# Attention with stationary values and sums divided in the transposes, evictions on ScalarE and split mLSTM cells, in a two-layer diffusion trunk

## What is computed

```python
def step(carry, xs):                       # mLSTM, one chunk of 128 tokens, one direction
    C, n, m = carry
    b = jnp.cumsum(fc, axis=-1)
    d = jnp.where(lower, b[..., :, None] - b[..., None, :] + ic[..., None, :], -jnp.inf)
    inter = b + m[..., None]
    m_t = jnp.maximum(inter, jnp.max(d, axis=-1))
    w = jnp.exp(d - m_t[..., None]) * jnp.einsum('bhtd,bhsd->bhts', qc, kc)
    a = jnp.exp(inter - m_t)
    num = a[..., None] * jnp.einsum('bhtd,bhdv->bhtv', qc, C) + jnp.einsum('bhts,bhsv->bhtv', w, vc)
...
def one_block(qblk):                       # attention
    s = jnp.einsum('bkgqd,bksd->bkgqs', qblk, k, preferred_element_type=jnp.float32) * scale
    p = jax.nn.softmax(s, axis=-1).astype(v.dtype)
    return jnp.einsum('bkgqs,bksd->bkgqd', p, v)
...
act = jax.nn.gelu(jnp.einsum('tped,td->tpe', u[eidx], xb), approximate=False)   # PEER
return jnp.einsum('tpe,tped->td', g * act, v[eidx])
```

## Time and profile before

| | before |
|---|---|
| median of 3 runs | 2664.69 us (2655.25 to 2669.79) |
| profiled execution | 2655.81 us, span 2654.0 us |
| TensorE matmuls busy | 1909.4 us (72%) |
| VectorE busy | 1847.1 us (70%) |
| ScalarE busy | 604.0 us (23%) |
| GpSimd busy | 861.5 us (32%) |
| gathers | 110592 packets, 805.36 MB, 74.5% of 16 DMA engines |
| all DMA | 958.15 MB, mean 361 GB/s |
| granted TensorE clock | 0.846 |

### The profile page before, as it was taken

One profiled execution on the slowest core, in us unless ns is written; L12 is line 12 of the kernel. 1 busy time (PEld: TensorE's weight loads), 2 busy tenths in 40 slices (PEclk: granted clock), 3 DMA queues, 4 the chain that ended last, 5 costly groups with the idle time before them and its releaser, 6 DMA issues. The chain is left out here.

```text
span 2654.0 us, 22937 instructions
## 1 busy us (share of the span) xinstructions
PE 1909.4 (72%) x6742; PEld 1103.9 (42%) x6742; DVE 1847.1 (70%) x4569; ACT 604.0 (23%) x1668; POOL 861.5 (32%) x772
## 2 busy tenths in 40 slices
PE   6686687588687666678877667488867776766665
PEld 5466354366354223344534335245534332322222
DVE  1325876686686897166688863988688779687765
ACT  2212322332121221122321221233211112211121
POOL 0001332233323443134334322344333444444432
PEclk8787888799788787678889878799879898888888
DMA  9755798679898999979899978799999999999996
GB/s 404 284 202 238 264 367 327 229 306 371 336 392 358 405 403 387 381 310 421 359 420 420 415 302 340 282 388 387 358 374 421 419 385 421 422 409 422 419 421 266
DMA packets 141040, 958.15 MB, mean 361 GB/s; under 512 B 19701, under 2 KB 21749, under 8 KB 25717
## 3 DMA queue, kind: packets, MB, share of 16 engines
q0 software_dynamic: 110592, 805.36, 74.5%
q1 hardware_dynamic: 23024, 147.01, 14.0%
q10 hardware_dynamic: 7300, 4.33, 0.5%
HBM read 953.75 MB, written 2.89 MB: 360 GB/s over the span
## 5 line engine op out<-in xcount | busy, mean ns | idle before, releaser
L677 PE MATMUL acc<-rows,diag 128*128 128x512 f32 x2136 | 1160.6, 695 | 453.1 <-ACT diag L853 452.7
L608 POOL DMA_INDIRECT rows<-in_uv,eidx x768 | 861.3, 1121 | 1754.0 <-PE acc L677 1220.8
L1135 DVE CUSTOM_DVE_ANT_0 rows<-rows,xb 128x1024 f32<-128x1024 f32 x768 | 917.7, 1222 | 259.6 <-DMA rows<-in_uv,eidx 259.0
L677 PEld LDWEIGHTS acc<-rows,diag 128*128 128x128 f32 x2136 | 454.3, 223 | 1074.8 <-ACT diag L853 571.4
L853 ACT ACTIVATE act_out<-act_in 128x2 f32<-128x2 f32 x384 | 78.1, 203 | 1448.5 <-DVE act_in L1135 1448.2
L1124 DVE SCALAR_TENSOR_TENSOR side<-rows,wv,side 128x1024 f32<-128x1024 f32 x234 | 300.7, 1285 | 8.4
L853 ACT ACT_TABLE_LOAD x138 | 177.1, 1283 | 133.8 <-DVE st L1088 33.7
L626 PE MATMUL bank<-wt,hT 128*128 128x256 f32 x896 | 200.0, 384 | 8.1 <-ACT hT L853 7.5
L853 ACT ACTIVATE diag<-small,wv 128x128 f32<-128x128 f32 x534 | 191.8, 387 | 0.0
L626 PEld LDWEIGHTS bank<-wt,hT 128*128 128x128 f32 x896 | 172.8, 193 | 39.2 <-ACT hT L853 8.1
L626 PE MATMUL bank<-hT,wt 128*128 128x256 f32 (+1 forms) x960 | 179.5, 348 | 4.5 <-ACT hT L853 3.7
(11 more groups left out here) (161 smaller groups left out, 1329.3 us busy)
## 6 DMA issues: line engine op xcount, KB each, us to landing
wt<-in_ada_w SPq DMA_DIRECT2D x27, 1024.0 KB, 10.9
wt<-in_peer_w_q SPq DMA_DIRECT2D x26, 1024.0 KB, 9.5
rows<-in_ada_w SPq DMA_DIRECT2D x21, 1024.0 KB, 19.6
wt<-in_mlstm_w_in SPq DMA_DIRECT2D x14, 1024.0 KB, 7.6
rows<-in_uv,eidx POOLq DMA_INDIRECT x768, 12.9
wt<-in_attn_w_qkv SPq DMA_DIRECT2D x12, 1024.0 KB, 9.5
rows<-in_mlstm_w_in SPq DMA_DIRECT2D x10, 1024.0 KB, 27.6
wt<-in_attn_w_out SPq DMA_DIRECT2D x8, 1024.0 KB, 9.7
```

What stands on the lines that cost most here:

```text
L608: nc.gpsimd.indirect_dma_start(out=rows[:, r, :], out_offset=None, in_=A["uv"], in_offset=bass.IndirectOffsetOnAxis(ap=eidx[:, b, slot:slo ...
L677: last = nc.tensor.matmul(acc[:, h * 512:(h + 1) * 512], diag[:, r, :], rows[:, r, D + h * 512:D + (h + 1) * 512], start=first and j == 0, ...
L1135: last = V.tensor_tensor_reduce(out=rows[:, r, 0:D], in0=rows[:, r, 0:D], in1=xb[:, place, :], scale=1.0, scalar=0.0, op0=ALU.mult, op1=AL ...
```

## The change

In words: (1) NT: both tiles go to ScalarE except for block 0 of layer 0. (2) PS: ScalarE copies the scores. (3) The steps MLA, MLB, MLC become MLD, MLW, MLA / MLB, MLE (two heads each) / MLC, MLK, MLU, with their own unit costs; MLB, MLE and MLU are late on VectorE, MLB and MLE on ScalarE. (4) AQ, a new step, squares q and k on ScalarE. (5) The rotary takes both axes in one operation. (6) A new step AR: VectorE inverts the sums, ScalarE makes a diagonal of each head's; AP is a product of prA with that diagonal; ScalarE copies the result; AV has the values stationary and two heads' probabilities moving, output by feature, which ScalarE copies into hT; T2 of layer 1 keeps only the gate. prA and the diagonals lie in the place of q in qkv.

```diff
@@ plan
-                yield ("MLA", g, d, b)
-                yield ("MLB", g, d, b)
+                yield from ((k, g, d, b) for k in ("MLD", "MLW", "MLA", "MLB", "MLE"))
                 if g == "P" or n < nb - 1:
-                    yield ("MLC", g, d, b)
+                    yield from ((k, g, d, b) for k in ("MLC", "MLK", "MLU"))
...
-        yield from (("AN", g, b) for b in range(nb))
+        for b in range(nb):
+            yield ("AQ", g, b)
+            yield ("AN", g, b)
         yield from (("AT", g, b) for b in range(nb))
-        yield from ((k, g, b, kv) for b in range(nb) for kv in range(AKV) for k in ("AS", "AP", "AV"))
+        yield from ((k, g, b, kv) for b in range(nb) for kv in range(AKV) for k in ("AS", "AR", "AP", "AV"))
@@ cost
-        return {"MLQK": 13, "MLV": 13, "MLO": 13, "OUT": 13, "PQ": 13, "AQKV": 13, "AS": 4, "AP": 5, "AV": 5, "MOD": 10}.get(s[0], 0) / (2 - both) \
-            or {"MLA": 8, "MLG": 8, "MLN": 10, "PS": 4, "PC": 5, "PG": 7, "PT": 5, "AN": 15, "CONV": 6, "NT": 4}.get(s[0], 6)
+        return {"MLQK": 13, "MLV": 13, "MLO": 13, "OUT": 13, "PQ": 13, "AQKV": 13, "AS": 4, "AR": 2, "AP": 5, "AV": 4, "MOD": 10}.get(s[0], 0) / (2 - both) \
+            or {"MLD": 4, "MLW": 4, "MLA": 4, "MLB": 4, "MLE": 5, "MLC": 3, "MLK": 2, "MLU": 5, "MLG": 8, "MLN": 10, "PS": 4, "PC": 5, "PG": 7, "PT": 5, "AQ": 1, "AN": 14, "CONV": 6, "NT": 4}.get(s[0], 6)
@@ in_order
-    late = {"P": (), "A": ("NT", "MLQK", "MLV", "MLO", "AQKV", "PQ", "OUT", "T2", "PS", "AS"),
-            "D": ("NT", "MLQK", "MLV", "MLO", "AQKV", "PQ", "OUT", "T2", "PS", "MOD", "AS", "AP", "AV")}[who]
+    late = {"P": (), "A": ("NT", "MLQK", "MLV", "MLO", "AQKV", "PQ", "OUT", "T2", "PS", "MLB", "MLE", "AS", "AP", "AV"),
+            "D": ("NT", "MLQK", "MLV", "MLO", "AQKV", "PQ", "OUT", "T2", "PS", "MLB", "MLE", "MLU", "MOD", "AS")}[who]
@@ psum_tiles
     if k == "NT":
-        return "AD"
+        return "AD" if nt_shared(s) else "AA"
...
     if k == "PS":
-        return "D" if s[4] else "DAA"
+        return "A" if s[4] else "AAA"
...
     if k == "AP":
-        return "DDDD"
+        return "AAAA"
     if k == "AV":
-        return "D"
+        return "A"
@@ TensorE
                 elif k == "AP":
                     _, g, b, kv = s
                     nk = 1 if g == "P" else 3
+                    pe.wait_ge(sums_diag, next_of(sums_diag))
                     for i in range(4):
-                        transposes(open_tile(i), [prA[i][:, c * P:(c + 1) * P] for c in range(nk)]).then_inc(tile_full, 1)
+                        t = open_tile(i)
+                        for c in range(nk):
+                            last = mm(t[:, c * P:(c + 1) * P], prA[i][:, c * P:(c + 1) * P], dgA[i], True, True)
+                        last.then_inc(tile_full, 1)
                 elif k == "AV":
...
-                    for i in range(4):
+                    for i in range(2):
                         for c in range(nk):
...
-                            last = mm(out[:, i * HD:(i + 1) * HD], prA[i][:, c * P:(c + 1) * P], v, c == 0, c == nk - 1)
+                            pair = qkv[:, 0:2, (3 * i + c) * P:(3 * i + c + 1) * P]
+                            last = mm(out[i * HD:(i + 1) * HD, 0:2 * P], v, pair, c == 0, c == nk - 1)
@@ ScalarE
+                elif k == "AQ":
+                    f(sq20, qkv[:, s[2], 0:(AH + AKV) * HD], ACT.Square).then_inc(squares, 1)
...
+                elif k == "AP":
+                    _, g, b, kv = s
+                    n = P if g == "P" else 3 * P
+                    for i in range(4):
+                        copy_tile(i, prA[i][:, 0:n], n)
+                elif k == "AR":
+                    act.wait_ge(sums_inverted, next_of(sums_inverted))
+                    for i in range(4):
+                        last = f(dgA[i], ident, ACT.Copy, scale=rrs[:, i:i + 1])
+                    last.then_inc(sums_diag, 1)
+                elif k == "AV":
+                    _, g, b, kv = s
+                    copy_tile(0, hT[:, 2 * kv:2 * kv + 2, tok(b)], 2 * P, lambda t: t.rearrange("p (q n) -> p q n", n=P))
@@ VectorE
+                elif k == "AR":
+                    V.reciprocal(rrs, rsum).then_inc(sums_inverted, 1)
```

More of the change, by code:

```diff
@@ L215, in psum_tiles @@
         return "DD"
+    if k == "MLD":
+        return "DD"
     if k == "MLA":
-        return "DDA"
-    if k == "MLB":
-        return "AD" * MH if s[1] == "S" else "D" * MH
+        return "A"
+    if k in ("MLB", "MLE"):
+        return "AD" * 2 if s[1] == "S" else "D" * 2
     if k == "MLC":
-        return "D" * (1 + MH)
+        return "D"
+    if k == "MLU":
+        return "D" * MH
     if k == "T2":
-        return "A" * (2 * len(BLOCKS[s[2]]) + 2)
+        return "A" * (2 * len(BLOCKS[s[2]]) * (s[1] == 0) + 2)
     if k == "OUT":
@@ L321, in needed @@
         return after("T2")
-    if s[0] == "PS" and who != "D":
+    if s[0] == "PS" and who == "P":
         return after("PQ")
@@ L485, in places @@
             for s in PLAN:
-                before.append((len(owner), total["A"], total["D"], total["acts"], total["dves"]))
+                held = {"MLW": 2, "MLA": 1, "MLK": 1}.get(s[0], 0)
+                before.append((len(owner), total["A"], total["D"] - held, total["acts"], total["dves"]))
                 for e in psum_tiles(s):
@@ L497, in begin @@
                 s = PLAN[i]
-                if s[0] in (*IDLE[who], "GROUPS") or (s[0] == "PS" and who == "A" and s[4]):
+                if s[0] in (*IDLE[who], "GROUPS") or (s[0] == "MLU" and who == "A" and s[1] == "S"):
                     return 0, 0, 0, 0, 0
@@ L750, in _ @@
                     last.then_inc(tile_full, 1)
-                elif k == "MLA":
+                elif k == "MLD":
                     _, g, d, b = s
@@ L920, in _ @@
                     c = COND[b]
[L921 to L922 removed]
                     place = tok(b - (b > 0))
[L924 to L927 removed]
+                    for i in range(1 if nt_shared(s) else 2):
+                        act.wait_ge(tile_full, full(i))
+                        t = tile(i)
+                        for q in range(4):
+                            e = 4 * i + q
+                            last = f(hT[:, e, place], t[:, q * P:(q + 1) * P], ACT.Identity,
+                                     scale=gain[:, l, w, e, c:c + 1], bias=modT[:, l, 24 * w + e, c:c + 1])
+                        last.then_inc(act_freed, 1)
                 elif k == "MLQK":
@@ L964, in _ @@
                     last.then_inc(probs_raw, 1)
-                    copy_tile(2, WT.rearrange("p h n -> p (h n)"))
-                elif k == "MLB":
+                elif k == "MLA":
+                    copy_tile(0, WT.rearrange("p h n -> p (h n)"))
+                elif k in ("MLB", "MLE"):
                     if s[1] == "S":
                         act.wait_ge(act_chain, noted())
-                        for h in range(MH):
-                            act.wait_ge(tile_full, full(2 * h))
-                            t = tile(2 * h)
+                        for i in range(2):
+                            h = i + 2 * (k == "MLE")
+                            act.wait_ge(tile_full, full(2 * i))
+                            t = tile(2 * i)
                             f(Nn[:, h, :], t[:, 0:DV + 1], ACT.Copy, scale=ae[:, h:h + 1]).then_inc(act_freed, 1)
@@ L1504, in _ @@
-                        last.then_inc(dve_step, 1)
+                        x1, x2, t1, t2 = wr[:, :, :, 0, :], wr[:, :, :, 1, :], t[:, 0], t[:, 1]
+                        cc, ss = [cst(n)[:, b * 32:b * 32 + 32].rearrange("p (a n) -> p a n", n=16).unsqueeze(1)
+                                  .to_broadcast([P, heads, 2, 16]) for n in ("cos", "sin")]
+                        V.tensor_tensor(t1, x1, ss, ALU.mult).then_inc(dve_chain, one())
+                        V.tensor_tensor(t2, x2, ss, ALU.mult).then_inc(dve_chain, one())
```

162 lines of the change are left out of this document (73 added, 89 removed).

## The result

The changed kernel takes 2669.47 us (median of 20 runs, 2646.55 to 2676.98), the kernel before 2657.14 us in the 20 runs beside it; the ratio is 1.0037, 95% interval [1.0019, 1.0055]. Forecast was 2654 us, a gain of 11 us; measured is a loss of about 10 us. By the bound of 0.5% that I had set for myself this is within no change, but the interval lies on the slower side alone, and that is the other sign. The range (2620 to 2686) held it. The kernel before, with 2664.69 as the median of its first three runs, has 2655 to 2660 us in every later set of 20 and more, so the 9 us that I added for the distance of profile and median were an accident of three runs.

The account below looks back on a forecast made before the run. Bounds: gathers at the DMA limit in the last 664 us, nearly so in attention; VectorE's work and waits in the sample's mLSTM cells. Terms -20 + 1 + 2 + 0 + 10 - 1 - 3 = -11 us: 2645, plus 9, 2654 us; range 2620 to 2686.

Parts of the forecast that it names:

- Sample cells, -20: Sample's mLSTM cells: groups between the split steps cover 21 us of VectorE's waits; with shifted groups and evictions, -20 us.
- Rival 4: mLSTM cells: MLE waits for MLB's emptied tiles, so the numerator's one wait becomes two; -1 us, 2664 us, chance 0.10.
- Prompt, +1: Prompt's mLSTM cells: no groups cover waits, and MLE waits for MLB's tiles, about 0.5 us in two cells; +1 us.
- NT, +2 (0 to +9): NT copies all on ScalarE: TensorE's next product up to 1.8 us later in five places, mostly behind groups; +2 us.
- Score tiles, 0 (-6 to +6): Score copies moved from VectorE to ScalarE, 24 tiles, ready at VectorE's next need give or take 1 us; 0.
- Attention core, +10: Sample's attention core: TensorE's loop, lengthened by reciprocal, diagonals and products for transposes, becomes the longer one; +10 us (-4 to +30).
- AQ and rotary, 0: Squares on ScalarE, which VectorE awaits instead of doing them; twelve rotary operations become six of twice the size; 0.
- Prompt attention and T2, -1 and -3: Prompt attention: AV's wait and copies leave VectorE, -1 us; T2 of layer 1 loses transposes and their copies, -3 us.
- rival 5: Attention core: transposes cost a quarter of a product, so products in their place cost more; +10 us, 2675 us, chance 0.03.

Follow-up runs that it names:

- the split kernel: The kernel before with only the mLSTM cells split (MLD to MLU, unit costs, late lists): 2648.17 us, ratio 0.9953.
- loosened conditions: Split cells alone, but MLE's products wait only for the W transposes and MLW's reduction only for the decay tile: 2635.19 us, ratio 0.9910 to the kernel before.
- two others of the same code: The changed kernel with the attention core as before, 2665.35 us (1.0013); the changed kernel with cached keys and values issued at the sample's first projection, 2649.87 us (0.9982).
- the early transfer: Cached keys and values issued at the sample's first projection, not behind the third; as the only edit to the kernel before: 2642.16 us, ratio 0.9955.

## Why the prediction was wrong

The sign was wrong because two costs of the change were put at almost nothing: the begin conditions that the split adds in the prompt (+1), and NT on one engine (+2).

- **Sample cells, -20: the size right, the sum behind it in part luck.** From the first gather to the start of (0,1) the split kernel gains 17.4 us (+16.1 to -1.3), and with loosened conditions 20.6 (+1.3 to -19.3). The changed kernel gains 8.9 (+10.3 to +1.4), as NT and the score tiles, each by itself, lose 8.7 and 6.8 in the same stretch. Rival 4 was right in its place: the numerator's wait stays (7.7 for 8.2) and TensorE's products add 6.6, so the waits fell by 13 us and not by 21. The gain is the other waits and the groups, up to 30 us by group 48, of which 10 are given back in the rest of the stage.
- **Prompt, +1: the step that failed first.** I costed the new wait of MLE alone, at 0.5 us a cell. The split also puts a begin condition in front of MLW, and both cost TensorE idle time in a stretch without groups. Measured at the first gather +10 in the changed kernel's profile (+4 and +5 in two others of the same code), +16 in the split alone, 15 of it these two conditions.
- **NT, +2 (0 to +9): the second.** "Groups lie in front of most of them" was wrong: the product follows within 0.10 us in four of six places, and the two blocks of the sample follow one another, so both differences count. The price of a block was wrong the other way: I had up to 1.8 us, and it is 0.65, as eight copies of 0.45 overlap and take 2.88 on one engine, and two engines need 2.24. Measured +12 (7 to 15) against a bound of 9, of which 7.3 are seen ahead of the products. That ScalarE is busy a quarter of the span said nothing about it.
- **Score tiles, 0 (-6 to +6):** +5, inside the bounds.
- **Attention core, +10: mechanism right, size near.** Spacing 18.9 us in the changed kernel against 18.1 forecast and 16.0 before (15.9 in the forecast); 18 us lost between groups 16 and 48 of (1,0), where I had taken 8 us off for copies and groups and expected 10. VectorE stands 1.96 us (forecast 1.9), the 24 instructions take 4.6 us in the mean by their weight loads (forecast 2.8 at full clock and 5.4 at half, half of them each, that is 4.1): seven of eight ran wholly or in part at the half clock. TensorE's wait ahead of them is 4.9 in the mean (forecast 5). AV was cheaper: 12 instructions of 256 columns behind 64 stationary ones take 2.00 us, 0.17 each; I had 0.23 from a row with 128. By the ratios the part costs 3 us, or 8 where the transfer of the cache does not blur it: less than the core loses. T2 and the prompt's core may give some back; that was not measured.
- **AQ and rotary, 0: right.** Prompt attention and T2, -1 and -3, were not measured by themselves.
- **The Trainium skill's rule.** "TensorE: Matmul & The Clock Gate", section Terms, gives the transpose mode as 4x faster for FP32, which I took as against a product. 12 transposes in 2.79 us and 24 instructions, which are 12 products, in 5.46 us, both at a granted clock of 0.50, are a factor of two; rival 5 falls.

Put right, the sum is -20 + 10 + 12 + 5 + 10 - 1 - 3 = +13 us against +10 to +12 measured. Two terms of 1 and 2 us carry 19 of the 24 us between -11 and +13, the score tiles the rest, and none of the three lay in a stretch that I had read row by row. That the sum meets the measurement is in part luck: NT and the score tiles together measured 11 and not 17, the attention part 3 or 8 and not 10, and the parts by their ratios give +2 us (1.0006), or +6 with the attention part's price of 8. Part of that gap may be the wait for the cached keys and values, which the prediction did not count and which was long in some profiles and short in others: with the early transfer the product of the parts meets the whole (0.9979 against 0.9982). It is not shown run by run.

## What to carry to other kernels

A step split in parts waits at each part's begin for everything before it, and where no other work is interleaved nothing hides these waits (15 us here, in two cells): carry the conditions over tile by tile. Copies that a product follows at once are worth splitting over two engines, however idle the one engine looks (12 us here, with ScalarE busy 23% of the span). A transfer issued where it is needed was a wait of 14 to 17 us in most profiles of this kernel; look for waits on DMA first, before any part of the compute is redone. And read one profile as one execution: where two executions of equal code can differ by a wait of 11 us, the column of one trace does not explain a difference of medians.

## What the runs showed that I had not expected

The three transfers of the cache (128 KB each) landed 16.2 to 19.0 us after their issue in the kernel before, among gathers and weight loads, at a DMA share of 0.94 (1631 to 1651 us), and 4.3 to 4.8 us after it when issued three steps earlier, at a share of 0.69 (1583 to 1590 us). DMA issues of both kernels, 1560 to 1660 us (count, KB each, median us to landing):

```profile
arena<-in_cache_attn_k ACTq DMA_DIRECT2D x2, 128.0 KB, 17.1
arena<-in_cache_attn_v ACTq DMA_DIRECT2D x1, 128.0 KB, 19.0
```

```profile
arena<-in_cache_attn_k ACTq DMA_DIRECT2D x2, 128.0 KB, 4.4
arena<-in_cache_attn_v ACTq DMA_DIRECT2D x1, 128.0 KB, 4.8
```

The same bytes took four times the time by the place of their issue. The Trainium skill's "DMA: Bandwidth & Descriptors", section Rules for kernel authors, says to issue a transfer early and wait on it late; the runs agree, at 12 us for one place in the kernel before and 3 in the split with loosened conditions. A fixed start-up cost can be no longer than the shortest landing, 2.2 us in the whole change with the early transfer; the rest of the 16.2 to 19.0 us is something else. That it is the other traffic fits the two shares and was not tested by itself.
